# Two blocks' scores are held, their searches stand among the gathered rows, and the gates come two chunk pairs later

## The chip, the cores and the metric

The kernel runs on one core of one Trainium2 chip. The metric is the device time of one execution in microseconds (us), the median of three runs. The engines are named as in the profile: PE (TensorE), DVE (VectorE), ACT (ScalarE), POOL (GpSimd), SP (SyncE, which here issues the weights' transfers).

## What is computed

Two layers over 512 tokens of 1024 numbers, fp32. The first mixes by windowed attention and Fourier mixing, the second by a gated spatial unit; each is followed by an expert layer ("PEER"), and in this one the change lies:

```python
def peer_ffn(h, w_q, keys, u_tab, v_tab):
    # 512 tokens in blocks of 128; 8 heads, 2 sides, 128 keys a side, 16384 experts
    q = (xc @ w_q).reshape(PEER_BLOCK, PEER_HEADS, 2, PEER_KEY_DIM // 2)
    s = jnp.einsum("chsd,hskd->chsk", q, keys).astype(jnp.float32)
    top_s, top_i = lax.top_k(s, PEER_TOPK)                              # 16 of 128 a side
    cand = top_s[:, :, 0, :, None] + top_s[:, :, 1, None, :]
    best_s, best = lax.top_k(cand.reshape(...), PEER_TOPK)              # 16 of 256 pairs
    e = i1 * PEER_NKEYS + i2
    g = jax.nn.softmax(best_s, axis=-1)
    act = jax.nn.gelu(jnp.einsum("cd,chkd->chk", xc, u_tab[e]))
    return jnp.einsum("chk,chkd->cd", g * act, v_tab[e])
```

Each token uses 8 × 16 = 128 of the 16384 rows of `u_tab` and of `v_tab`.

## The kernel before

`peer_phase` builds one expert layer and is called twice. The 512 tokens are four blocks of 128. Blocks 0 and 1 are **gathered**: their rows are fetched from memory, 512 KB at a time. Blocks 2 and 3 are **dense**: for them PE multiplies by all experts, and a matrix of gates, zero nearly everywhere, picks out those that count.

**Asks.** For m = 0 to 15 (head and side) PE makes the query tile m of all four blocks (`ask(m)`, 24 matmuls) and then the scores: `score(m)` for blocks 0 to LATER−1, in one of two PSUM banks (L1243 and on), and `later_score(m)` for the last block. `score(m)` waits until DVE has replaced the found values of search m−2. DVE searches 16 of 128 twice: `top16(m)` takes blocks 0 to LATER−1 together, instruction by instruction; `later_top16(m)` takes the last block alone, from a copy that ACT made (`hold(m)`). Between searches DVE routes block 0 and part of block 1 (`route(b, step)`, 23 steps that find the best pairs and the experts' numbers; step 5 gives ACT the differences for the exponential of block b), and takes slots 0 to 7.

**Up.** For chunk c = 0 to 127 PE multiplies the two dense blocks by 128 experts' rows (`up(c)`), whose 512 KB come through a ring of three buffers that SP fills; ACT takes the result by `gelu(c)` into the matrix `gates`. `up(c)` waits for `gelu(c-2)`. After a pair of chunks p = c // 2 that stands in `EXP_AFTER`, ACT waits for the differences of a block and takes their exponential (L1553), in order with the gelus. After a pair in `TURN_AFTER` PE turns a dense block's weights, and DVE's `columns(b)` puts them where ACT can use them.

**Gates.** 32 groups of 8 tokens, 16 for each dense block. ACT makes one-hot rows (`one_hots`), PE multiplies them (`gates_of(g)`, L1300, at the pair in `GATES_AFTER`, one half behind each chunk), and the product, 8 × 128 × 128, says how much each expert counts. For chunks not yet computed ACT copies it into `gates` (`take_gates`, L1538), and gelus are later multiplied onto it (`post(p)` on DVE); for those already computed DVE multiplies (`spread(g)`, L1859). PSUM has room for two groups, so `gates_of(g)` waits for `spread(g-2)` and `take_gates(g-2)`.

**Down.** For c = 0 to 127 PE multiplies `gates` by the second table's rows (`down(c)`, L1310). It starts when all 32 groups are spread.

**Slots.** Beside all this DVE takes 512 slots, each one row per token for one block: 256 dots with `u_rows` (L1888) and 256 accumulations of `peer_v` rows (L1895). POOL fetches them by indirect transfers (L1134) into a dozen buffers and more; some (`EARLY`) lie in parts of `gates` that are not yet in use. What else DVE does after slot 7 is written out by slot numbers: behind slot i come `TOP_AT` (a single search), `ROUTE_AT`, `SOFTMAX_AT`, `COLUMNS_AT`, `SPREAD_AT` and `POST_AT`, in this order (L2050 to L2062). All engines run their instructions in program order. In layer 0, DVE's dense residual (L1960) stands between two of the last slots and opens the next layer's mixing; in layer 1 the last slots open the ending. The values of the tables before are in the diff.

Of the kernel before, what the change touches and what calls it, by code (L numbers as in the profile page):

```python
# [27 lines left out]
P = 128  # L28
# [19 lines left out]
FETCHED = 2  # L48
LATER = 3
PICKED = FETCHED * P  # L50
# [742 lines left out]
class Experts:  # L793


    def __init__(self, nc, room, l, split_at):
# [109 lines left out]
def peer_phase(nc, t, l, out_w, out_gate, xT, x_dram, hi, lo, ring, both, norm, ident, iota, one, gate, q,  # L906
               bridge=None, mixer=None, ending=None):

    with Room(nc, f"exp{l}") as r:
# [11 lines left out]
        FIRST_DOTS = 46  # L921
        EARLY = [(31, 0, 44), (39, 0, 60), (47, 0, 76), (55, 0, 88), (66, 60, 112), (74, 60, 128)]

        HEADS = [(0, 2), (2, 4), (4, PH)]
        ASK_ROUTE = {m: (0, range(8 * (m - 4), min(8 * (m - 4) + 8, STEPS))) for m in (4, 5, 6)}
        ASK_ROUTE.update({m: (1, range(8 * (m - 8), min(8 * (m - 8) + 8, STEPS))) for m in (8, 9, 10)})
        ASK_TOP = {1: 0, 2: 1, 3: 2, 7: 3}
        ASK_SLOTS = {11: (0, 1), 12: (2, 3), 13: (4, 5), 14: (6, 7)}
        SHIFT = 1 + ASK_SLOTS[14][1]
        FIRST_ROWS = 8  # L930

        GATES_AFTER = {13 + 3 * g // 2: g for g in range(GROUPS)}
# [15 lines left out]
        POST_AT = {SHIFT + (44 + 4 * (p - 14) if p <= 34 else 124 + 465 * (p - 34) // 100): p for p in POST}  # L948

# [230 lines left out]
        def _(pe):  # L1180
# [257 lines left out]
        def _(act):  # L1438
# [247 lines left out]
        def _(dve):  # L1686
# [349 lines left out]
            for i in range(SHIFT, SLOTS):  # L2036
# [6 lines left out]
                if ending and i == SLOTS - 3:  # L2043
# [203 lines left out]
```

## Time and profile before

| | |
|---|---|
| three runs | 2830.92, 2814.94, 2823.93 us |
| median | 2823.93 us |
| the profiled execution | 2829.58 us, its span 2827.5 us |
| PE busy | 2648.9 us, 94% |
| DVE busy | 2017.5 us, 71% |
| POOL busy | 1476.7 us, 52% |
| ACT busy | 1048.1 us, 37% |
| mean granted clock of PE | 0.976 |

All times of the trace count from the start of the span. The stages are, in layer 0 and layer 1:

| | layer 0 | layer 1 |
|---|---|---|
| up begins | 459 | 1790 |
| down begins | 979 | 2309 |
| PE's last tile down ends | 1450.5 | 2780.4 |
| last slot ends | 1511 | 2813 |

A row of a timeline gives the start, the length, the engine, the line, the operation, out<-in, how many of the same kind stand in a row, and in brackets the idle time before it with what ended it. A row of the view by lines gives busy time, mean length in ns and idle time before with what ended it. Since each engine works in order, the start of a row says when everything ahead of it on that engine was done.

### The profile page before, as it was taken

The numbers are of one execution on the slowest core, as the hardware profiler recorded it, in microseconds if no ns is written. First come the engines' busy times: TensorE is split into PE (matmuls) and PEld (weight loads), VectorE is DVE, ScalarE is ACT, GpSimd is POOL, SyncE is SP. The second block draws the span as 40 slices with busy tenths as digits, with TensorE's granted clock in tenths as the row PEclk, the third lists the DMA queues.
The fourth block names the chain that finished last, engine by engine and source line by source line (L and its number), as shares of the span: only waits on it lengthen the run. The fifth ranks groups of instructions, "written<-read, shape, count | busy, mean of one in ns | idle before, by whom it ended". The sixth has DMA issues, their size and how long they took to land. (4 is left out here: it accounts for less than half of the span.)

```text
span 2827.5 us, 37113 instructions
## 1 busy us (share of the span) xinstructions
PE 2648.9 (94%) x13042; PEld 2201.9 (78%) x13042; DVE 2017.5 (71%) x4301; ACT 1048.1 (37%) x2993; POOL 1476.7 (52%) x1122
## 2 busy tenths in 40 slices
PE   6899999999999999999978799999999999999996
PEld 4644687888888888888867778888888888888884
DVE  5463389988678756666677638998877775666667
ACT  4362331398888500000024432239878830000002
POOL 1000352656667745565647435365676774665554
PEclk9999999999999999999988999999999999999998
DMA  8282335999999999999985234699999999999997
GB/s 338 107 350 98 120 132 194 392 365 352 384 409 409 406 404 409 409 409 409 409 327 198 84 121 156 221 402 361 355 395 409 409 408 404 409 409 409 409 409 292
DMA packets 251625, 925.37 MB, mean 327 GB/s; under 512 B 27409, under 2 KB 35633, under 8 KB 244273
## 3 DMA queue, kind: packets, MB, share of 16 engines
q0 software_dynamic: 147456, 536.94, 48.4%
q1 hardware_dynamic: 99824, 381.88, 35.2%
q10 hardware_dynamic: 4160, 4.19, 0.4%
q8 instruction: 104, 1.70, 0.2%
q14 instruction: 81, 0.66, 0.1%
HBM read 916.61 MB, written 6.29 MB: 326 GB/s over the span
## 5 line engine op out<-in xcount | busy, mean ns | idle before, releaser
L1310 PE MATMUL exp_down<-peer_gates,all_ring 128*128 128x256 f32 x2720 | 612.8, 382 | 24.1 <-DMA all_ring<-in_peer_v 24.0
L1283 PE MATMUL exp_out<-peer_both,all_ring 128*128 128x256 f32 x2752 | 621.6, 382 | 7.8 <-DMA all_ring<-in_uT 5.1
L1310 PEld LDWEIGHTS exp_down<-peer_gates,all_ring 128*128 128x128 f32 x2720 | 509.4, 190 | 117.2 <-DMA all_ring<-in_peer_v 50.3
L1283 PEld LDWEIGHTS exp_out<-peer_both,all_ring 128*128 128x128 f32 x2752 | 519.6, 192 | 81.7 <-DMA all_ring<-in_uT 11.6
L1134 POOL DMA_INDIRECT all_xT<-in_u_rows,peer_eidx x278 | 365.9, 1316 | 157.0 <-DVE peer_dots L1888 91.2
L1895 DVE SCALAR_TENSOR_TENSOR peer_both<-all_xT,peer_dots,peer_both 128x1024 f32<-128x1024 f32 x226 | 299.9, 1327 | 148.1 <-DMA all_xT<-in_peer_v,peer_eidx 144.6
L1888 DVE CUSTOM_DVE_ANT_0 all_xT<-all_xT,peer_both 128x1024 f32<-128x1024 f32 x278 | 338.7, 1224 | 62.6 <-DMA all_xT<-in_u_rows,peer_eidx 61.2
L1134 POOL DMA_INDIRECT all_xT<-in_peer_v,peer_eidx x230 | 271.1, 1179 | 189.3 <-DVE peer_both L1895 156.7
L1310 PE MATMUL exp_down<-peer_gates,spare_ring 128*128 128x256 f32 x1376 | 315.1, 382 | 11.6 <-DMA spare_ring<-in_peer_v 11.5
L1521 ACT ACTIVATE spare_heavy<-all_iota_b,spare_index 128x128 f32<-128x128 bf16 x1024 | 314.3, 412 | 0.0
L1283 PE MATMUL exp_out<-peer_both,spare_ring 128*128 128x256 f32 x1344 | 304.8, 380 | 1.6 <-DMA spare_ring<-in_uT 1.5
L1895 DVE SCALAR_TENSOR_TENSOR peer_both<-late,peer_dots,peer_both 128x1024 f32<-128x1024 f32 x168 | 219.6, 1307 | 117.6 <-DMA late<-in_peer_v,peer_eidx 115.2
L1310 PEld LDWEIGHTS exp_down<-peer_gates,spare_ring 128*128 128x128 f32 x1376 | 257.6, 190 | 58.9 <-DMA spare_ring<-in_peer_v 25.0
L1283 PEld LDWEIGHTS exp_out<-peer_both,spare_ring 128*128 128x128 f32 x1344 | 251.2, 190 | 35.1 <-DMA spare_ring<-in_uT 3.6
L1134 POOL DMA_INDIRECT late<-in_peer_v,peer_eidx x168 | 189.7, 1129 | 142.7 <-DVE peer_both L1895 126.4
L1525 ACT ACTIVATE spare_heavy<-spare_heavy,spare_share 128x128 f32<-128x128 f32 x512 | 212.2, 503 | 0.0
L1607 ACT ACTIVATE bridge_w_hi<-bridge_raw 128x1024 fp32r<-128x1024 f32 x32 | 33.7, 1052 | 476.6 <-DMA bridge_raw<-in_w_gs_in 476.6
L1107 POOL TENSOR_TENSOR ask_w_lo<-ask_third,ask_w_hi 128x1024 fp32r<-128x1024 f32 x14 | 33.7, 2405 | 285.4 <-ACT ask_w_hi L1443 285.3
L1569 ACT ACTIVATE ending_gated<-exp_down,all_ada 128x256 f32<-128x256 f32 x8 | 3.0, 489 | 470.8 <-PE exp_down L1310 470.8
L1134 POOL DMA_INDIRECT peer_gates<-in_u_rows,peer_eidx x94 | 117.7, 1252 | 99.4 <-DVE peer_dots L1888 64.7
L125 PE MATMUL exp_down<-all_h_hi,ask_w_hi 128*128 128x512 f32 x352 | 145.2, 412 | 11.7 <-DVE ask_w_lo L1918 11.7
L1300 PEld LDWEIGHTS exp_down<-spare_heavy 128*128 128x128 f32 x1024 | 132.3, 192 | 26.4 <-ACT spare_heavy L1529 13.6
(323 smaller groups left out, 4161.8 us busy)
## 6 DMA issues: line engine op xcount, KB each, us to landing
all_ring<-in_uT SPq DMA_DIRECT2D x172, 512.0 KB, 6.8
all_ring<-in_peer_v SPq DMA_DIRECT2D x170, 512.0 KB, 6.8
mix_raw<-in_ada_tiles SPq DMA_DIRECT2D x48, 1024.0 KB, 10.3
spare_ring<-in_peer_v SPq DMA_DIRECT2D x86, 512.0 KB, 6.8
spare_ring<-in_uT SPq DMA_DIRECT2D x84, 512.0 KB, 6.8
bridge_raw<-in_w_gs_in SPq DMA_DIRECT2D x32, 512.0 KB, 3.5
all_ring<-in_w_peer_q SPq DMA_DIRECT2D x20, 512.0 KB, 3.4
ask_third<-in_w_peer_q SPq DMA_DIRECT2D x12, 512.0 KB, 3.5
```

The lines of the kernel that those rows point to most:

```text
L125: nc.tensor.matmul(out, w_hi, x_hi, start=first, stop=False)
L1107: nc.gpsimd.tensor_tensor(q.w_lo[m % 3][:, :, :], asked[m % 3][:, :, :], f32(q.w_hi[m % 3][:, :, :]), ALU.subtract).then_inc(s_lo, 1)
L1134: nc.gpsimd.indirect_dma_start(out=rows[j], out_offset=None, in_=t["u_rows"] if n < HALF else t["peer_v"], in_offset=bass.IndirectOffsetOn ...
L1283: mm = nc.tensor.matmul(outs[:, c % 2, 0:DENSE], raw[c % R][:, k, :], hd[:, k, :], start=(k == 0), stop=(k == KD - 1))
L1300: mm = nc.tensor.matmul(ps_g[g % 2][:, half * TG // 2 + k, :], heavy[:, 1, k, :], heavy[:, 0, k, :], start=True, stop=True)
L1310: mm = nc.tensor.matmul(dn[:, m, :], raw[at % R][:, m, :], gates[:, :, c, :], start=(c == 0 and m % 2 == 0), stop=(c == NKEYS - 1), skip_g ...
L1521: act.activation(heavy[:, side, k, :], iota[:, :, 0], ACT.Abs, scale=2.0, bias=q.index[:, b, side, first + k:first + k + 1]).then_inc(s_ap ...
L1525: act.activation(heavy[:, 0, k, :], heavy[:, 0, k, :], ACT.Relu, bias=q.share[:, b, 0, first + k:first + k + 1], scale=q.share[:, b, 1, fi ...
L1569: act.activation(ending.gated[:, m, :], dn[:, m, :], ACT.Copy, scale=gate[:, m:m + 1]).then_inc(s_egate, 1)
L1607: act.activation(bridge.w_hi[i % 3][:, :, :], bridge.raw[i % 3][:, :, :], ACT.Copy).then_inc(s_bhi, 1)
L1888: nc.vector.tensor_tensor_reduce(out=row, in0=row, in1=own[:, b, :], scale=1.0, scalar=0.0, op0=ALU.mult, op1=ALU.add, accum_out=q.dots[:, ...
L1895: nc.vector.scalar_tensor_tensor(out=acc[:, b, :], in0=row, scalar=q.dots[:, b, k:k + 1], in1=acc[:, b, :], op0=ALU.mult, op1=ALU.add).the ...
```

## The change

`LATER` falls from 3 to 2. `top16(m)` now searches blocks 0 and 1 only. The scores of blocks 2 and 3 are both held: `later_score(m)` is two matmuls, `hold(m)` two copies, and the new tensor `held` lies where `weighed` lay. `later_top16` takes the block as an argument, so there are 32 single searches in a layer in place of 16. Six of block 2's stand in the asks; its other ten are behind slots 8 to 17, and block 3's sixteen behind slots 42 to 57 (before: block 3's only, four in the asks and twelve behind every second slot of 33 to 55). Everything behind them moves: block 2's route from slots 8 to 30 to slots 18 to 40, its softmax from 31 to 41, its columns from 36 to 46, its spreads from 49, 54, 59 and so on to 61, 66, 71 and so on; block 3's first spread from 153 to 160 and its last from 255 to 262; block 1's route begins at slot 66 (58) and block 3's at 95 (90). On PE the gates of block 2 begin at pair 15 (13), those of block 3 at pair 39 (38). On ACT exp(0) stands after pair 0 (1) and exp(2) after pair 6 (4).

```diff
-LATER = 3
+LATER = 2
+        held = nc.alloc_sbuf_tensor_at(f"held{l}", [P, HS, NKEYS], F32, offset=weighed_at)
-        self.later_scores = later.sb("scores", [P, HS, NKEYS])
+        self.later_scores = [held, later.sb("scores", [P, HS, NKEYS])]
...
-        EARLY = [(31, 0, 44), (39, 0, 60), (47, 0, 76), (55, 0, 88), (66, 60, 112), (74, 60, 128)]
+        EARLY = [(31, 0, 44), (39, 0, 60), (47, 0, 76), (55, 0, 88), (66, 66, 112), (74, 66, 128)]
-        ASK_TOP = {1: 0, 2: 1, 3: 2, 7: 3}
+        ASK_TOP = {1: (2, 0), 2: (2, 1), 3: (2, 2), 7: (2, 3), 12: (2, 4), 13: (2, 5)}
-        GATES_AFTER = {13 + 3 * g // 2: g for g in range(GROUPS)}
-        GATES_AFTER.update({38 + 3 * g // 2: GROUPS + g for g in range(GROUPS)})
+        GATES_AFTER = {15 + 3 * g // 2: g for g in range(GROUPS)}
+        GATES_AFTER.update({39 + 3 * g // 2: GROUPS + g for g in range(GROUPS)})
-        EXP_AFTER = {1: 0, 4: 2, 20: 1, 28: 3}
-        TURN_AFTER = {9: 2, 33: 3}
+        EXP_AFTER = {0: 0, 6: 2, 20: 1, 28: 3}
+        TURN_AFTER = {11: 2, 34: 3}
-        ROUTE_AT = {SHIFT + n: (2, n) for n in range(STEPS)}
-        ROUTE_AT.update({SHIFT + 50 + 13 * n // 10: (1, n) for n in range(STEPS)})
-        ROUTE_AT.update({SHIFT + 82 + 13 * n // 10: (3, n) for n in range(STEPS)})
-        TOP_AT = {SHIFT + 25 + 2 * (m - 4): m for m in range(4, HS)}
-        SOFTMAX_AT = {SHIFT + 3: 0, SHIFT + 23: 2, SHIFT + 81: 1, SHIFT + 113: 3}
-        COLUMNS_AT = {SHIFT + 28: 2, SHIFT + 121: 3}
-        SPREAD_AT = {SHIFT + 41 + 5 * g + g * g // 15: g for g in range(GROUPS)}
-        SPREAD_AT.update({SHIFT + 145 + 68 * g // 10: GROUPS + g for g in range(GROUPS)})
+        ROUTE_AT = {SHIFT + 10 + n: (2, n) for n in range(STEPS)}
+        ROUTE_AT.update({SHIFT + 58 + 12 * n // 10: (1, n) for n in range(STEPS)})
+        ROUTE_AT.update({SHIFT + 87 + 13 * n // 10: (3, n) for n in range(STEPS)})
+        TOP_AT = {SHIFT + n: [(2, 6 + n)] for n in range(HS - 6)}
+        TOP_AT.update({SHIFT + 34 + n: [(3, n)] for n in range(HS)})
+        SOFTMAX_AT = {SHIFT + 3: 0, SHIFT + 33: 2, SHIFT + 86: 1, SHIFT + 118: 3}
+        COLUMNS_AT = {SHIFT + 38: 2, SHIFT + 128: 3}
+        SPREAD_AT = {SHIFT + 53 + 5 * g + g * g // 15: g for g in range(GROUPS)}
+        SPREAD_AT.update({SHIFT + 152 + 68 * g // 10: GROUPS + g for g in range(GROUPS)})
...
             def later_score(m):
...
-                score_block(m, LATER, later[m % 2]).then_inc(s_later_score, 1)
+                for i in range(NB - LATER):
+                    mm = score_block(m, LATER + i, later[m % 2][:, i, :])
+                mm.then_inc(s_later_score, 1)
...
             def hold(m):
                 act.wait_ge(s_later_score, m + 1)
-                act.activation(q.later_scores[:, m, :], later[m % 2], ACT.Copy).then_inc(s_held, 1)
+                for i in range(NB - LATER):
+                    last = act.activation(q.later_scores[i][:, m, :], later[m % 2][:, i, :], ACT.Copy)
+                last.then_inc(s_held, 1)
```

(`POST_AT` moves likewise, by 10 slots; `SHIFT` is 8, `STEPS` 23, `HS` and `GROUPS` 16.)

Three places in the order of instructions. The first is DVE in the asks of layer 0 at m = 12 (`top16`, and in the kernel after it `later_top16`): `exp_ps_t` is the PSUM tensor with the scores, `top_val` the found values. Before:

```order
L1709 MAX top_val<-exp_ps_t 128x8 x3
L1712 MAX_INDEX ask_idx<-top_val,exp_ps_t 128x8 x3
L1714 MATCH_REPLACE ask_kept<-top_val,exp_ps_t 128x128 x3
L1718 MAX top_val<-ask_kept 128x8 x3
L1721 MAX_INDEX ask_idx<-top_val,ask_kept 128x8 x3
L1723 CAST top_idx_2693<-ask_idx 128x3x32
```

After:

```order
L1716 MAX top_val<-exp_ps_t 128x8 x2
L1719 MAX_INDEX ask_idx<-top_val,exp_ps_t 128x8 x2
L1721 MATCH_REPLACE ask_kept<-top_val,exp_ps_t 128x128 x2
L1725 MAX top_val<-ask_kept 128x8 x2
L1728 MAX_INDEX ask_idx<-top_val,ask_kept 128x8 x2
L1730 CAST top_idx_2694<-ask_idx 128x2x32
L1737 MAX top_val<-held_2681 128x8
L1739 MAX_INDEX later_idx<-top_val,held_2681 128x8
L1740 MATCH_REPLACE later_kept<-top_val,held_2681 128x128
L1743 MAX top_val<-later_kept 128x8
L1745 MAX_INDEX later_idx<-top_val,later_kept 128x8
L1747 CAST top_idx_2694<-later_idx 128x32
```

The three-block search has become a two-block one, and behind six of the sixteen a search of six instructions for block 2 alone has come.

The second is DVE from slot 8 on (`ISA` is a slot's dot, the row with `peer_dots 128x1` its result), layer 0. Before, block 2's route starts at once:

```order
L1888 ISA spare_row,peer_dots<-spare_row,peer_both 128x1024
L1888 ISA peer_dots 128x1
L1759 TENSOR_TENSOR top_cand<-top_val 128x8x16
L1761 TENSOR_TENSOR top_cand<-top_val 128x8x56
L1764 TENSOR_TENSOR top_cand<-top_val 128x8x8
L1888 ISA all_xT,peer_dots<-all_xT,peer_both 128x1024
L1888 ISA peer_dots 128x1
L1769 MAX top_best<-top_cand 128x8 x8
```

After:

```order
L1895 ISA spare_row,peer_dots<-spare_row,peer_both 128x1024
L1895 ISA peer_dots 128x1
L1737 MAX top_val<-held_2681 128x8
L1739 MAX_INDEX later_idx<-top_val,held_2681 128x8
L1740 MATCH_REPLACE later_kept<-top_val,held_2681 128x128
L1743 MAX top_val<-later_kept 128x8
L1745 MAX_INDEX later_idx<-top_val,later_kept 128x8
L1747 CAST top_idx_2694<-later_idx 128x32
L1895 ISA all_xT,peer_dots<-all_xT,peer_both 128x1024
L1895 ISA peer_dots 128x1
```

Ten slots with a search of block 2 each have come ahead of its route.

The third is ACT at the start of the up stage of layer 0 (`exp_out` is PSUM with a chunk's result, `top_less` the differences). Before:

```order
L1501 ACT_TABLE_LOAD
L1501 ACTIVATE peer_gates<-exp_out 128x2x128 x4
L1553 ACT_TABLE_LOAD
L1553 ACTIVATE top_less<-top_less 128x128
L1501 ACT_TABLE_LOAD
L1501 ACTIVATE peer_gates<-exp_out 128x2x128 x6
L1553 ACT_TABLE_LOAD
L1553 ACTIVATE top_less<-top_less 128x128
L1501 ACT_TABLE_LOAD
L1501 ACTIVATE peer_gates<-exp_out 128x2x128 x15
```

After:

```order
L1508 ACT_TABLE_LOAD
L1508 ACTIVATE peer_gates<-exp_out 128x2x128 x2
L1560 ACT_TABLE_LOAD
L1560 ACTIVATE top_less<-top_less 128x128
L1508 ACT_TABLE_LOAD
L1508 ACTIVATE peer_gates<-exp_out 128x2x128 x12
L1560 ACT_TABLE_LOAD
L1560 ACTIVATE top_less<-top_less 128x128
L1508 ACT_TABLE_LOAD
L1508 ACTIVATE peer_gates<-exp_out 128x2x128 x15
```

The exponential of block 2 stands behind 14 gelus, where it stood behind 10.

## Rows read from the trace of the kernel before

**Rows 1.** By lines, PE, 371 to 460 us; then timeline, PE.
```profile
L1241 PE MATMUL exp_ps_t<-ask_keys,ask_qT 128*128 128x128 f32 x84 | 12.6, 288 | 6.6 <-DVE ask_kept L1714 6.6
...
410.04 0.83 PE L1241 MATMUL exp_ps_t<-ask_keys,ask_qT 128*128 128x128 f32 x6
...
1788.94 0.91 PE L1241 MATMUL exp_ps_t<-ask_keys,ask_qT 128*128 128x128 f32 x6 [0.55 <-DVE ask_kept L1714]
```

**Rows 2.** Timeline, PE, two tiles up of layer 0.
```profile
467.83 3.62 PE L1283 MATMUL exp_out<-peer_both,spare_ring 128*128 128x256 f32 x16
471.29 1.03 PE L1283 MATMUL exp_out<-peer_both,all_ring 128*128 128x256 f32 x4
```

**Rows 3.** Timeline, ACT, layer 0, the exponential of block 2.
```profile
499.54 0.31 ACT L1553 ACTIVATE top_less<-top_less 128x128 f32<-128x128 f32 x1 [2.19 <-DVE top_less L1775]
```

**Rows 4.** Timeline, DVE, the first spread of layer 0 and of layer 1.
```profile
567.06 0.38 DVE L1859 TENSOR_TENSOR peer_gates<-peer_gates,exp_down 128x224 f32<-128x224 f32 x1
...
1898.96 0.38 DVE L1859 TENSOR_TENSOR peer_gates<-peer_gates,exp_down 128x224 f32<-128x224 f32 x1
```

**Rows 5.** Timeline, PE, the third group of gates in both layers.
```profile
581.76 1.05 PE L1300 MATMUL exp_down<-spare_heavy 128*128 128x128 f32 x8
...
1913.43 1.05 PE L1300 MATMUL exp_down<-spare_heavy 128*128 128x128 f32 x8
```

**Rows 6.** By lines, DVE, 585 to 722 us; then timeline, spreads of groups 2 and 12.
```profile
L1859 DVE TENSOR_TENSOR peer_gates<-peer_gates,exp_down 128x272 f32<-128x272 f32 (+10 forms) x11 | 6.1, 558 | 22.4 <-ACT peer_gates L1538 22.4
...
590.84 0.44 DVE L1859 TENSOR_TENSOR peer_gates<-peer_gates,exp_down 128x272 f32<-128x272 f32 x1 [3.76 <-ACT peer_gates L1538]
...
719.34 0.69 DVE L1859 TENSOR_TENSOR peer_gates<-peer_gates,exp_down 128x512 f32<-128x512 f32 x1 [5.60 <-ACT peer_gates L1538]
```

**Rows 7.** Windows of L1895: window, us, DVE busy (x), clock, DMA, GB/s; timeline, last spread.
```profile
979.00:1450.00 471.00, 296.98 (x232) 1.00 1.03 408
...
976.54 1.17 DVE L1859 TENSOR_TENSOR peer_gates<-peer_gates,exp_down 128x976 f32<-128x976 f32 x1
```

**Rows 8.** Timeline, PE and DVE, both layers' ends; then window of L1895, DVE.
```profile
1446.91 3.62 PE L1310 MATMUL exp_down<-peer_gates,all_ring 128*128 128x256 f32 x16
...
1455.75 1.65 DVE L1960 SCALAR_TENSOR_TENSOR back<-exp_down,all_ada,back 128x256 f32<-128x256 f32 x4
...
2776.75 3.62 PE L1310 MATMUL exp_down<-peer_gates,all_ring 128*128 128x256 f32 x16
...
2780.40:2813.30 32.90, 28.42 (x21) 0.81 0.69 270
```

**Rows 9.** Timeline, DVE: searches in the asks, slot 8, a single search, layer 1.
```profile
381.74 0.68 DVE L1709 MAX8 top_val<-exp_ps_t 128x8 f32<-128x128 f32 x3
...
385.58 0.28 DVE L1730 MAX8 top_val<-later_scores 128x8 f32<-128x128 f32 x1
...
416.17 0.69 DVE L1709 MAX8 top_val<-exp_ps_t 128x8 f32<-128x128 f32 x3
...
483.37 1.22 DVE L1888 CUSTOM_DVE_ANT_0 spare_row<-spare_row,peer_both 128x1024 f32<-128x1024 f32 x1
...
530.73 1.22 DVE L1888 CUSTOM_DVE_ANT_0 peer_gates<-peer_gates,peer_both 128x1024 f32<-128x1024 f32 x1
...
531.88 0.29 DVE L1730 MAX8 top_val<-later_scores 128x8 f32<-128x128 f32 x1
...
533.67 1.22 DVE L1888 CUSTOM_DVE_ANT_0 peer_gates<-peer_gates,peer_both 128x1024 f32<-128x1024 f32 x1
...
1749.24 0.70 DVE L1709 MAX8 top_val<-exp_ps_t 128x8 f32<-128x128 f32 x3
...
1815.28 1.22 DVE L1888 CUSTOM_DVE_ANT_0 spare_row<-spare_row,peer_both 128x1024 f32<-128x1024 f32 x1
```

**Rows 10.** Timeline, PE, after a wait in the mixing; then its window, columns as above.
```profile
1480.20 0.58 PE L125 MATMUL exp_out<-bridge_h_hi,bridge_w_hi 128*128 128x256 f32 x1 [6.36 <-POOL bridge_w_lo L1160]
...
1480.20:1483.50 3.30, 3.30 (x15) 0.50 0.76 226
```

More of the change, by code:

```diff
@@ L812, in __init__ @@
         self.first_pick = asks.sb("first_pick", [P, PH // 2, TOPK, TOPK], BF16)
+        weighed_at = asks.at
         self.weighed = [asks.sb(f"weighed{j}", [P, KD, P]) for j in range(2)]
+        held = nc.alloc_sbuf_tensor_at(f"held{l}", [P, HS, NKEYS], F32, offset=weighed_at)
         self.moved = asks.sb("moved", [P, 2, 2])
@@ L930, in peer_phase @@
         FIRST_ROWS = 8
-        GATES_AFTER = {13 + 3 * g // 2: g for g in range(GROUPS)}
-        GATES_AFTER.update({38 + 3 * g // 2: GROUPS + g for g in range(GROUPS)})
+        GATES_AFTER = {15 + 3 * g // 2: g for g in range(GROUPS)}
+        GATES_AFTER.update({39 + 3 * g // 2: GROUPS + g for g in range(GROUPS)})
         DONE_AFTER = {g: 2 * p + 2 for p, g in GATES_AFTER.items()}
         WEIGH_AFTER = {p - 1: g for p, g in GATES_AFTER.items()}
-        EXP_AFTER = {1: 0, 4: 2, 20: 1, 28: 3}
-        TURN_AFTER = {9: 2, 33: 3}
-        ROUTE_AT = {SHIFT + n: (2, n) for n in range(STEPS)}
-        ROUTE_AT.update({SHIFT + 50 + 13 * n // 10: (1, n) for n in range(STEPS)})
-        ROUTE_AT.update({SHIFT + 82 + 13 * n // 10: (3, n) for n in range(STEPS)})
-        TOP_AT = {SHIFT + 25 + 2 * (m - 4): m for m in range(4, HS)}
-        SOFTMAX_AT = {SHIFT + 3: 0, SHIFT + 23: 2, SHIFT + 81: 1, SHIFT + 113: 3}
-        COLUMNS_AT = {SHIFT + 28: 2, SHIFT + 121: 3}
-        SPREAD_AT = {SHIFT + 41 + 5 * g + g * g // 15: g for g in range(GROUPS)}
-        SPREAD_AT.update({SHIFT + 145 + 68 * g // 10: GROUPS + g for g in range(GROUPS)})
+        EXP_AFTER = {0: 0, 6: 2, 20: 1, 28: 3}
[9 more added lines that the diff above has]
+        SPREAD_AT.update({SHIFT + 152 + 68 * g // 10: GROUPS + g for g in range(GROUPS)})
         POST = [p for p in range(PAIRS) if p > min(GATES_AFTER)]
-        POST_AT = {SHIFT + (44 + 4 * (p - 14) if p <= 34 else 124 + 465 * (p - 34) // 100): p for p in POST}
+        POST_AT = {SHIFT + (54 + 4 * (p - 16) if p <= 36 else 134 + 465 * (p - 36) // 100): p for p in POST}
         def known(p):
@@ L988, in peer_phase @@
         query = [dn[:, 2 * j:2 * j + 2, :].rearrange("p m n -> p (m n)") for j in range(2)]
-        later = [dn[:, 4 + 2 * j, 0:NKEYS] for j in range(2)]
+        later = [dn[:, 4 + 2 * j, :].rearrange("p (b n) -> p b n", n=NKEYS) for j in range(2)]
         turned = [outs[:, :, :].rearrange("p j n -> p (j n)"), dn[:, 4:8, :].rearrange("p m n -> p (m n)")]
@@ L1724, in top16, with later_top16 @@
                                                q.idx[:, :, :].unsqueeze(3).broadcast_to([P, LATER, TOPK, 2])))
-            def later_top16(m):
-                found, val = q.later_scores[:, m, :], q.val[:, LATER, m, :]
+            def later_top16(b, m):
+                found, val = q.later_scores[b - LATER][:, m, :], q.val[:, b, m, :]
                 dve.wait_ge(s_held, m + 1)
@@ L1739, in later_top16 @@
                 settled()
-                mark(nc.vector.tensor_copy(q.idx2[:, LATER, m % 2, m // 2, :, :],
+                mark(nc.vector.tensor_copy(q.idx2[:, b, m % 2, m // 2, :, :],
                                            q.later_idx[:, :].unsqueeze(2).broadcast_to([P, TOPK, 2])))
-                if m == HS - 1:
+                if (b, m) == (NB - 1, HS - 1):
                     settled()
@@ L1947, in _ @@
                 if m in ASK_TOP:
-                    later_top16(ASK_TOP[m])
+                    later_top16(*ASK_TOP[m])
                 if m in ASK_ROUTE:
@@ L2047, in _ @@
                     nc.vector.reciprocal(ending.rstd0[:, :], ending.rstd0[:, :]).then_inc(s_erstd0, 1)
-                if i in TOP_AT:
-                    later_top16(TOP_AT[i])
+                for b, m in TOP_AT.get(i, ()):
+                    later_top16(b, m)
                 if i in ROUTE_AT:
```

## The prediction

> **What bounds the kernel now.** I read the windows by stage, then waits at the seams of each expert layer. Both layers run the same program: the asks (16 tiles of queries and scores), 128 tiles up, 128 tiles down, and beside them 512 slots of gathered rows on VectorE (DVE).
>
> *Asks.* DVE searches without a pause while TensorE (PE) has to wait for it: 6.6 us in layer 0, 0.55 us before the last scores of layer 1 [rows 1]. PE's next tile starts when these scores are out, so DVE's searches are on the path in layer 0 and level with PE in layer 1.
>
> *Up stage, until the first spread.* PE sets the pace, one tile each 471.29 − 467.83 = 3.46 us [rows 2]. Three things come to it from DVE's slot table: the differences for exp(2) (ACT waits for them, and gelus queue behind it), the columns, and the spreads, since `gates_of(2)` on PE waits for `spread(0)`. In the trace exp(2) waits 2.19 us [rows 3]; `spread(0)` is 14.7 us ahead of `gates_of(2)` (567.06 against 581.76 us, 1898.96 against 1913.43) [rows 4, 5]. After it DVE is the early one: it waits 22.4 us for ACT's gates in 585 to 722 us, although it has done all it was given [rows 6].
>
> *Down stage.* DMA is full (share 1.03, 408 GB/s), and the rows come at 471 / 232 = 2.03 us a slot where DVE needs 1.3 [rows 7]. The last spread stands at 976.54 us, some 2 us ahead of the down stage, which begins at 979 [rows 7].
>
> *Ends.* Layer 0 ends by the slot that opens the dense residual: PE's last tile is done at 1446.91 + 3.62 = 1450.5, the residual starts at 1455.75 [rows 8]. Layer 1 ends by gathered rows: PE is done at 2780.4, then 21 accumulations take 28.42 us, 1.35 each [rows 8].
>
> **The change, part by part.** *Searches in the asks.* A search of three blocks takes 385.58 − 381.74 = 3.84 us [rows 9]. For two blocks the trace has no row; the bounds are 2/3 of it, 2.56, and all of it, 3.84. I take 2.75, near 2/3, since every instruction in it is one of three equal ones: −1.1 us each. A single search takes 533.67 − 531.88 = 1.79, and the dot ahead of it 531.88 − 530.73 = 1.15 [rows 9]. From the ninth search to slot 8 DVE takes 67.2 us in layer 0 and 66.0 in layer 1 [rows 9]. Now it is eight searches × −1.1 = −8.8, and two singles more × 1.79 = +3.6: −5.2. In layer 0 that search also starts when PE's scores are ready, 410.8, not at 416.17 [rows 1, 9]. Slot 8: 410.8 + 62.0 = 472.8 (10.6 earlier); layer 1: 1749.1 + 60.8 = 1809.9 (5.4 earlier). PE's asks lose their waits: −6.6 and −0.55. The extra score and copy per ask are the same four matmuls on PE and one more short copy on ACT, which has nothing else there: nothing.
>
> *Searches among the slots.* 26 stand there instead of 12; until the first spread it is 25 (slots 8 to 17, 42 to 56) instead of 8, and `spread(0)` stands 12 slots later. Before: 567.06 − 483.37 = 83.7 us from slot 8 [rows 4, 9]. Now 83.7 + 12 × 1.15 + 17 × 1.79 = 127.9. So `spread(0)` starts at 472.8 + 127.9 = 600.7 in layer 0 (33.6 later) and 1937.8 in layer 1 (38.8 later).
>
> *Gates two pairs later.* That is four tiles, 4 × 3.46 = 13.8 us. PE without a stall comes to `gates_of(2)` at 581.76 − 6.6 + 13.8 = 589.0 and 1913.43 − 0.55 + 13.8 = 1926.7 [rows 1, 2, 5]. `spread(0)` ends 0.4 after its start, at 601.1 and 1938.2: **12.1 and 11.5 us short**. Tables that gave 14.7 us of room now give none.
>
> *exp(2).* Its differences came 499.54 − 483.37 = 16.2 us behind slot 8 [rows 3, 9]. They now stand behind ten slots and ten searches more: 16.2 + 11.5 + 17.9 = 45.6, at 518.4 and 1855.5. Tile 16 needs the gelu that is queued behind exp(2), done about 2 us after the differences (estimated from the trace's function load and one gelu): 520.4 and 1857.5. Without a wait tile 16 would start at 467.83 + 14 × 3.46 − 6.6 = 509.7 [rows 2], and in layer 1, where up starts at about 1789.35, at 1844.7 [rows 1]. PE stands 10.7 and 12.8 us. This is not added to the 12.1 and 11.5: a PE that stood there comes to `gates_of(2)` at 599.7 and 1939.5, about when `spread(0)` ends. The two waits are one, and the longer rules: PE is late by −6.6 + 12.1 = +5.5 in layer 0 and −0.55 + 12.8 = +12.3 in layer 1.
>
> *Clock.* Behind 6.36 us of standing, 15 matmuls take 3.30 us at a granted clock of 0.50, 1.2 GHz [rows 10]; at 1.00 they would take half: about 1.6 us lost. Two such stops, the second partly inside the same wait: +1.8. For exp(1)'s differences (slot 72, some 11 slots and three spreads behind `spread(0)`, about 622, level with tile 41) I add 1. PE goes down **8.3 us later in layer 0 and 15.1 in layer 1**.
>
> The Trainium skill ("TensorE: Matmul & The Clock Gate", section "Part 1: The HAM clock gate") says that an idle array falls to 1.2 GHz and gets 2.4 GHz back only after sustained work. It speaks against this change, which puts stops into a stage that had none of this length; the trace agrees in kind (0.50 behind the 6.36 us).
>
> *Gathered rows.* From `spread(2)` at slot 59 to `spread(12)` at slot 118 a slot took (719.34 − 590.84) / 59 = 2.18 us, paced by the gates [rows 6]. The spreads stand 12 slots later, 26.1 us at that pace; the gates come 13.8 + 8.3 = 22.1 and 13.8 + 15.1 = 28.9 us later. The stream is thus 4.0 us ahead in layer 0 and 2.8 behind in layer 1, and the buffers have time to fill before. Bounds: no row gained, and 7 (the 14.7 us of room at 2.03). I take three rows in layer 0 and two in layer 1, near the low end. Block 3's spreads stand 7 slots later, its gates one pair: 14.2 us (at 2.03) against 6.9 + 8.3 or + 15.1, so the last spread stays about level with PE.
>
> *Sum.* Layer 0: PE's end 1450.5 + 8.3 = 1458.8 now decides, since the slot that opened the residual at 1455.75 comes no later: +3.1. Layer 1: while PE is at work a slot costs 2.03, after it 1.35, so 15.1 us more of PE leave 1 − 1.35 / 2.03 = 0.33 of it: +5.0; two rows gained: −2.7. Together +3.1 + 2.3 = **+5.4**. The profiled execution took 2829.58 (span 2827.5), 5.65 above the median 2823.93: 2835.0, or **2829** as a median.
>
> **The rivals.** *No change.* The stops are as forecast but made good: slot 491 had 5.2 us of room over PE, and more rows come during the stops. With four rows more in layer 1 (−5.4) and PE 5 late in layer 0 it is +0; about 2824. For it: DVE's 22.4 us of waiting, which the searches now fill. Against: that room lies after `spread(0)`, the stops before it.
>
> *Faster.* Searches are cheaper alone than I count. The low bound is a third of a three-block search, 1.28: 17 × 0.51 = 8.7 us, and with two-block searches at 2.56 another 1.5 us; PE then waits 2 us. PE keeps its 6.6, the slot stream the room. Layer 0: PE no longer waits, slot 491 comes by PE's end, −5.2; layer 1: eight rows (14.7 us and what the asks give) × 1.35 = −10.8. About 2824 − 16 = 2808. For it: DVE idles later. Against: the single searches wait on one another, and 1.79 is measured.
>
> *Slower.* Place: the seam from up to down, some 2 us wide [rows 7]. Block 3's spreads stand seven slots later at up to 2.03 us each, 14.2 us; the gates come one pair later. If DVE has gained no row by slot 118 and instead lags three (dots behind 26 searches, block 1 and 3's routes from slot 66 and 95 close behind), the last spread, slot 262, is 14.2 + 3 × 2.03 = 20.3 later, at 996.8, and done at 998, 19 behind the 979 of before. Layer 0: 19 − 5.2 = +14; layer 1: 19 × 0.33 + 3 × 1.35 = +10. About 2824 + 24 = 2848. It decides once DVE lags by more than those 2 us and PE's own delay. For it: a search more costs DVE 1.79 in a stage with 12 more of them. Against: 22.4 us of waits per layer to take it from. A two-block search as dear as three (3.84) leads here too: 8.8 us more on both stops.
>
> **How the numbers follow.** Forecast as worked out, 2829: 0.50. No change, 2824: 0.22. Faster, 2808: 0.13. Slower, 2848: 0.15. A measurement of this kernel tells 0.5% from no change, 14 us; so the first two are "same", 0.72, faster 0.13, slower 0.15. The range takes in both outer cases, with two us more on the side where all of layer 0's gain would show: 2806 to 2848.
>
> **What would show it.** Slot 8 at about 473 and 1810 us: the searches' price. ACT's exp(2) waiting some 15 us, and PE standing before tile 16: the exp step. PE's `gates_of(2)` at 601 and 1938 with little wait of its own: the two waits are one. DVE's waits for gates in 600 to 750 us falling from 22.4 to under 15: the cover. PE's first tile down at 987 in layer 0 (979 before), the last spread ahead of it. The dense residual at 1459, straight behind PE. In layer 1, 20 to 25 accumulations behind PE's last tile. I am wrong if PE does not stand before tile 16 or `gates_of(2)`, if the last spread comes behind PE's last tile up, or if the rows behind PE's end number under 15 or over 30.

## The result, and the profile after

The changed kernel takes 2846.68 us (median of five runs, 2845.17 to 2852.63) against 2823.93: the ratio is 1.0093, 95% interval 1.0079 to 1.0108. It is slower by 23 us. I had given "no measurable change" 0.72 and put the likeliest time at 2829. The measured time lies at the upper end of the stated range, 2806 to 2848, next to the rival "slower"; how much of that rival's mechanism was right is said below. The profiled execution took 2851.54 us (span 2849.5), 22.0 us more than that of the kernel before, so its trace holds the whole difference.

PE's waits in layer 0, by line, what they waited for, total, times, longest (the view of waits, kernel after, 340 to 1500 us):

```profile
PE exp_down L1315 <- DMA all_ring<-in_peer_v: 12.9, 17, 1.1
PE exp_out L1288 <- ACT peer_gates L1508: 11.9, 2, 10.2
PE exp_down L1315 <- DVE peer_gates L1866: 7.4, 1, 7.4
```

Two are new: 10.2 us before tile 16 and 7.4 us before the first tile down. The kernel after, timeline of PE and ACT, layer 0 (L1288 is `up`, L1315 `down`, L1560 the exponential):

```profile
520.34 0.31 ACT L1560 ACTIVATE top_less<-top_less 128x128 f32<-128x128 f32 x1 [14.22 <-DVE top_less L1782]
...
522.49 1.62 PE L1288 MATMUL exp_out<-peer_both,all_ring 128*128 128x256 f32 x3 [10.19 <-ACT peer_gates L1508]
...
993.05 5.88 PE L1315 MATMUL exp_down<-peer_gates,spare_ring 128*128 128x256 f32 x16 [7.40 <-DVE peer_gates L1866]
```

The last row is one tile: 5.88 us where a tile takes 3.62 [rows 8]. The window behind it shows why (us, PE busy, granted clock, DMA share, GB/s):

```profile
992.00:997.00 5.00, 3.95 (x9) 0.50 1.03 410
```

DVE in the kernel after: the ninth slot, the first spread of either layer, the last spread of layer 0. They answer to [rows 4], [rows 7] and [rows 9]:

```profile
474.82 1.22 DVE L1895 CUSTOM_DVE_ANT_0 spare_row<-spare_row,peer_both 128x1024 f32<-128x1024 f32 x1
...
602.94 0.42 DVE L1866 TENSOR_TENSOR peer_gates<-peer_gates,exp_down 128x256 f32<-128x256 f32 x1
...
1947.93 0.42 DVE L1866 TENSOR_TENSOR peer_gates<-peer_gates,exp_down 128x256 f32<-128x256 f32 x1
...
991.77 1.18 DVE L1866 TENSOR_TENSOR peer_gates<-peer_gates,exp_down 128x992 f32<-128x992 f32 x1
```

And DVE's waits for gates in 600 to 750 us (by lines), 22.4 in the kernel before [rows 6]:

```profile
L1866 DVE TENSOR_TENSOR peer_gates<-peer_gates,exp_down 128x256 f32<-128x256 f32 (+12 forms) x13 | 7.2, 558 | 2.5 <-ACT peer_gates L1545 2.5
```

To see where time comes in, I compared when the same instruction starts in two traces. Minus means earlier than in the kernel before; all in us.

| place | after | block 3's spreads back | stop alone, in the kernel before |
|---|---|---|---|
| layer 0, tile 0 up | −5.9 | −4.2 | −3.0 |
| tile 14 | −5.0 | +1.0 | +13.9 |
| tile 20 | +6.8 | +11.5 | +14.0 |
| tile 127 | +6.8 | +5.2 | +12.9 |
| first tile down | +14.3 | +5.5 | +12.9 |
| tile 8 down | +16.4 | +5.2 | +12.7 |
| last tile down | +17.6 | +7.3 | +13.0 |
| dense residual | +12.5 | +2.2 | +11.8 |
| layer 1, tile 0 up | +8.2 | −0.3 | +10.6 |
| tile 127 | +19.4 | +11.0 | +26.3 |
| first tile down | +26.3 | +11.8 | +26.3 |
| last tile down | +28.9 | +11.0 | +26.6 |
| last slot | +22.1 | +11.3 | +27.3 |

In the kernel after each layer gets about 12 us at the stop before tile 16, another 7 at the seam, and about 2 at the low clock behind it. Rows get ahead of PE while it stands at the seam: slot 491 of layer 0 comes 9.2 us earlier than in the kernel before, with block 3's spreads back 0.9 later. So the ends give some back: layer 0's residual stood 5.2 us behind PE's end and stands straight behind it now, the mixing behind it takes 4.4 us less (+12.5 becomes +8.2), and layer 1 has fewer rows left behind PE:

```profile
2809.30:2835.30 26.00, 14.79 (x11) 0.91 0.33 127
```

This window of L1902 in the kernel after answers to the one of [rows 8]: 11 accumulations where there were 21. DVE then waits 7.4 us for the ending's scale, which comes from PE's last tile over ACT (the view of waits, 2809 to 2836 us):

```profile
DVE ending_rstd L2052 <- ACT ending_rstd L1596: 7.4, 1, 7.4
```

So the end of layer 1 hung on gathered rows before, and hangs on PE's last tile now.

### The profile page after: what moved, and what is told of

Read it like the earlier page. It is cut to its first block and busy times, and to the rows that moved or that the text cites. A ratio compares the mean times of both kernels' runs of the same rounds, so it can differ in the third digit from the quotient of the medians.

```text
span 2849.5 us, 37189 instructions
## 1 busy us (share of the span) xinstructions
PE 2654.3 (93%) x13042; PEld 2197.8 (77%) x13042; DVE 2036.2 (71%) x4329; ACT 1052.3 (37%) x3021; POOL 1434.9 (50%) x1122
## 5 line engine op out<-in xcount | busy, mean ns | idle before, releaser
L1288 PE MATMUL exp_out<-peer_both,all_ring 128*128 128x256 f32 x2752 | 626.9, 382 | 30.3 <-ACT peer_gates L1508 23.2
L1315 PE MATMUL exp_down<-peer_gates,all_ring 128*128 128x256 f32 x2720 | 612.4, 382 | 22.6 <-DMA all_ring<-in_peer_v 22.4
L1315 PEld LDWEIGHTS exp_down<-peer_gates,all_ring 128*128 128x128 f32 x2720 | 508.7, 190 | 115.8 <-DMA all_ring<-in_peer_v 47.9
L1288 PEld LDWEIGHTS exp_out<-peer_both,all_ring 128*128 128x128 f32 x2752 | 515.8, 191 | 105.8 <-issue 24.7
L1137 POOL DMA_INDIRECT all_xT<-in_u_rows,peer_eidx x280 | 349.7, 1249 | 203.6 <-DVE peer_dots L1895 149.9
L1902 DVE SCALAR_TENSOR_TENSOR peer_both<-all_xT,peer_dots,peer_both 128x1024 f32<-128x1024 f32 x228 | 302.5, 1327 | 153.5 <-DMA all_xT<-in_peer_v,peer_eidx 149.0
L1895 DVE CUSTOM_DVE_ANT_0 all_xT<-all_xT,peer_both 128x1024 f32<-128x1024 f32 x280 | 340.2, 1220 | 61.8 <-DMA all_xT<-in_u_rows,peer_eidx 60.5
L1315 PE MATMUL exp_down<-peer_gates,spare_ring 128*128 128x256 f32 x1376 | 319.7, 386 | 28.5 <-DMA spare_ring<-in_peer_v 14.6
L1315 PEld LDWEIGHTS exp_down<-peer_gates,spare_ring 128*128 128x128 f32 x1376 | 260.0, 192 | 78.8 <-DMA spare_ring<-in_peer_v 29.3
L1288 PE MATMUL exp_out<-peer_both,spare_ring 128*128 128x256 f32 x1344 | 304.1, 379 | 1.4 <-ACT peer_gates L1516 1.3
L1902 DVE SCALAR_TENSOR_TENSOR peer_both<-late,peer_dots,peer_both 128x1024 f32<-128x1024 f32 x168 | 219.5, 1307 | 108.3 <-DMA late<-in_peer_v,peer_eidx 105.2
L1288 PEld LDWEIGHTS exp_out<-peer_both,spare_ring 128*128 128x128 f32 x1344 | 252.8, 190 | 35.1 <-issue 1.7
L1305 PE MATMUL exp_down<-spare_heavy 128*128 128x128 f32 x1024 | 137.9, 278 | 13.0 <-issue 7.8
```

Of the source, the lines that this page charges most:

```text
L1137: nc.gpsimd.indirect_dma_start(out=rows[j], out_offset=None, in_=t["u_rows"] if n < HALF else t["peer_v"], in_offset=bass.IndirectOffsetOn ...
L1288: mm = nc.tensor.matmul(outs[:, c % 2, 0:DENSE], raw[c % R][:, k, :], hd[:, k, :], start=(k == 0), stop=(k == KD - 1))
L1305: mm = nc.tensor.matmul(ps_g[g % 2][:, half * TG // 2 + k, :], heavy[:, 1, k, :], heavy[:, 0, k, :], start=True, stop=True)
L1315: mm = nc.tensor.matmul(dn[:, m, :], raw[at % R][:, m, :], gates[:, :, c, :], start=(c == 0 and m % 2 == 0), stop=(c == NKEYS - 1), skip_g ...
L1895: nc.vector.tensor_tensor_reduce(out=row, in0=row, in1=own[:, b, :], scale=1.0, scalar=0.0, op0=ALU.mult, op1=ALU.add, accum_out=q.dots[:, ...
L1902: nc.vector.scalar_tensor_tensor(out=acc[:, b, :], in0=row, scalar=q.dots[:, b, k:k + 1], in1=acc[:, b, :], op0=ALU.mult, op1=ALU.add).the ...
```

## The experiments

Ratios are against the kernel before, measured again beside each variant; its medians there were 2821.8 to 2824.4 us.

**The seam undone.**

```diff
-        SPREAD_AT.update({SHIFT + 152 + 68 * g // 10: GROUPS + g for g in range(GROUPS)})
+        SPREAD_AT.update({SHIFT + 145 + 68 * g // 10: GROUPS + g for g in range(GROUPS)})
```

> The changed kernel with one table entry undone: block 3's spreads stand behind slots 153 to 255 again, not 160 to 262. Seam theory (the last spread, paced by rows that come at 2.03 us a slot, holds PE's first tile down): PE's wait there falls from 7.4 us to under 1, layer 0 goes down at about 985.5 instead of 993.05, PE ends both down stages 8 to 9 us earlier, the whole is 2831 (2828 to 2835). Stop theory (PE's stop of 10.2 us before tile 16 is what costs): nothing of the 22.8 us comes back, 2846 +- 4.

Measured: 2839.38 us, ratio 1.0059 (1.0037 to 1.0081); profiled span 2838.8, 10.7 under that of after. PE has no wait for the last spread; down begins at 984.28. Seven slots of one table are worth 7.3 us by the medians (5.2 if each is taken against the kernel before measured beside it) and 10.7 by the profiles, as the seam theory wants in sign and place, though less than the 15 it gave. The stop before tile 16 (9.1 us) is left, and now layer 1 loses by it 11.6 us from first tile to last slot.

**The seam added to the kernel before**: the same entry the other way, 145 to 152.

> The kernel before with one table entry changed: block 3's spreads stand behind slots 160 to 262. Seam theory: last spread 14 us later, at about 990.7, PE waits about 12 us for it, goes down at about 992 at half clock for a few us, residual of layer 0 about 10 us later, layer 1's end 7 to 8 later still: 2841 (2836 to 2846). Stop theory: no stop is added before the spreads, so 2824 to 2827.

Measured: 2863.3 us, 1.0145 (1.0120 to 1.0170). Far more than expected. PE's waits in layer 0 (view of waits, 400 to 1500 us; L1300 is `gates_of`) and one of them:

```profile
PE exp_down L1300 <- issue: 19.4, 6, 8.3
...
792.27 1.62 PE L1300 MATMUL exp_down<-spare_heavy 128*128 128x128 f32 x6 [8.27 <-issue]
```

Here `gates_of(18)` stands where it stood while `spread(16)`, which it waits for, comes at 791.37 and takes 0.80 us, seven slots later; and so on with five more groups. The view names no releaser for these waits; that it is the spread follows from the program and from the times. The last spread then comes no later than PE does, and there is no wait at the seam. In the changed kernel the gates stand one pair later; PE waits only 5.5 us of this kind in layer 0 (3.5 in the kernel before), and the seven slots are felt at the seam instead. The price of slots depends on which of the two waits PE meets.

**The stop moved away, the seam left.** Block 3's searches behind slots 62 to 77, exp(2) and the turn later:

```diff
-        EARLY = [(31, 0, 44), (39, 0, 60), (47, 0, 76), (55, 0, 88), (66, 66, 112), (74, 66, 128)]
+        EARLY = [(31, 0, 44), (39, 0, 60), (47, 0, 76), (55, 0, 88), (66, 84, 112), (74, 84, 128)]
-        EXP_AFTER = {0: 0, 6: 2, 20: 1, 28: 3}
-        TURN_AFTER = {11: 2, 34: 3}
+        EXP_AFTER = {0: 0, 9: 2, 20: 1, 28: 3}
+        TURN_AFTER = {13: 2, 34: 3}
-        TOP_AT.update({SHIFT + 34 + n: [(3, n)] for n in range(HS)})
+        TOP_AT.update({SHIFT + 54 + n: [(3, n)] for n in range(HS)})
```

> The changed kernel without its stop: block 3's single searches stand behind slots 62 to 77 instead of 42 to 57 (28.6 us less ahead of the first spread), exp(2) after pair 9 and the turn after pair 13, block 3's spreads stay at slots 160 to 262. Seam theory: PE's wait before tile 16 (10.2) goes, its last tile up ends 11 to 13 us earlier, and the wait for the last spread grows from 7.4 to about 19; down still begins at about 993, the whole stays at 2846 +- 4. Stop theory: 10 us a layer come back, 2826 to 2830.

Measured: 2869.1 us, 1.0169 (1.0148 to 1.0189), 22 slower than after; both theories missed it. The wait before tile 16 did go, but the searches now stand between the spreads, and PE and ACT wait there (waits of PE in 400 to 1500 us, of ACT in 600 to 700):

```profile
PE exp_down L1305 <- issue: 14.6, 8, 5.6
...
PE exp_down L1315 <- DVE peer_gates L1866: 7.1, 1, 7.1
...
ACT top_less L1560 <- DVE top_less L1782: 10.7, 1, 10.7
```

The seam's 7.1 stayed as it was, since rows and spreads fell back together.

**Both at once**: the last edit and the spreads back at 145.

> Both at once: no stop (block 3's searches behind slots 62 to 77, exp(2) after pair 9, turn after pair 13) and block 3's spreads back behind slots 153 to 255. Seam theory: the last spread stands at 976 to 977 as in the kernel before, PE waits 4 to 6 us for it and goes down at about 978 to 980; the 6.6 us from the asks are lost there; 2824 (2818 to 2829), level with the kernel before. Stop theory: as without the seam, 2826 to 2830, no better than the same kernel with the late spreads.

Measured: 2852.89 us, 1.0109 (1.0089 to 1.0128). Not level with before: the expectation failed with its premise, that moving the searches would free PE. Against the last kernel the seam is worth 16.2 us here.

**The stop moved, no search moved** (seam undone, `EXP_AFTER` 6 to 9, `TURN_AFTER` 11 to 13).

> The kernel with block 3's spreads back at slots 153 to 255, and besides exp(2) after pair 9 (was 6) and the turn of block 2 after pair 13 (was 11); no search is moved. If the stop before tile 16 and a stop for the first spread are one and the same lateness of DVE (as the prediction had it), the wait before tile 16 (9.1 us) goes and PE waits 8 to 14 us at the gates of group 2 for the first spread instead; down begins within 1 us of where it did (984.3 in layer 0), 2839 +- 4. If the exponential's place is the cause by itself, PE is 9 us earlier and the time is 2828 to 2832.

Measured: 2840.58 us, 1.0070 (1.0042 to 1.0098), the same as the 2839.38 with the stop in its old place. The wait before tile 16 is gone; in its place PE waits for the first spread before the gates of group 2:

```profile
601.18 1.19 PE L1305 MATMUL exp_down<-spare_heavy 128*128 128x128 f32 x4 [6.43 <-issue]
```

Its other waits for gates in that stretch make up a part (2.5 us for the one-hots of group 0). That the exponential and the spread show one lateness of DVE, and not two costs, holds, with a wait of 6.4 where I gave 8 to 14: from the first tile up to the last tile down PE loses 11.2 and 11.4 us in the two layers, against 11.5 and 11.4 with the stop in its old place.

**The searches left out.** The 26 single searches among the slots are not made; their results are zeros, set once. First with the spreads late, then with the spreads back.

```diff
+            mark(nc.vector.memset(q.val[:, LATER:NB, :, :], 0.0))
+            mark(nc.vector.memset(q.idx2[:, LATER:NB, :, :, :, :], 0.0))
...
                 for b, m in TOP_AT.get(i, ()):
-                    later_top16(b, m)
+                    if (b, m) == (NB - 1, HS - 1):
+                        settled()
+                        dve.sem_inc(s_later, 1)
```

> The changed kernel without the 26 single searches among the slots (that part of the computation is left out, their results are zeros set once), everything else in its place, block 3's spreads at slots 160 to 262. DVE loses 46 us of work a layer. Seam theory in its strict form (only the slot number of the last spread counts, since rows are paced by DMA): PE has no stop in the up stage and waits 10 to 18 us for the last spread; down begins at 988 to 993 in layer 0; 2838 to 2846. Search theory (the searches' time is the cost, wherever the spreads stand): PE's stop and the seam wait both go, 2818 to 2826.

> The same without the 26 searches, and block 3's spreads back at slots 153 to 255. If the loss of the change is the sum of two things, the seam (7 slots) and DVE's 17 more searches before the first spread (PE's stop), neither is left: level with the kernel before or up to 8 us below it, 2814 to 2824. If it is over 2830, something else in the change costs, for instance the gates standing later on PE.

Measured: 2836.18 us, 1.0043 (1.0030 to 1.0057), and 2820.68 us, 0.9993 (0.9980 to 1.0006). The seam stands alone in the first, the second has neither. The start of the down stage in the first and in the second:

```profile
984.53 1.19 PE L1315 MATMUL exp_down<-peer_gates,spare_ring 128*128 128x256 f32 x2 [7.37 <-DVE peer_gates L1866]
```

```profile
975.52 1.75 PE L1315 MATMUL exp_down<-peer_gates,spare_ring 128*128 128x256 f32 x7 [0.74 <-DVE peer_gates L1866]
```

The four kernels make a table, medians in us, with the spans of the profiles in brackets:

| | spreads at 160 to 262 | at 153 to 255 | the seam |
|---|---|---|---|
| 26 searches among the slots | 2846.7 (2849.5) | 2839.4 (2838.8) | 7.3 (10.7) |
| none of them | 2836.2 (2834.3) | 2820.7 (2821.7) | 15.5 (12.6) |
| the searches | 10.5 (15.2) | 18.7 (17.1) | both: 26.0 (27.8) |

By the medians either cause would hide 8 us of the other, but the upper two kernels were each measured apart from the lower two, and single runs of the one with 2839.4 reach from 2831.9 to 2848.2. The traces show no hiding. PE's wait at the seam in layer 0 is 7.40 us with the searches and 7.37 without. From the first tile up to the last tile down the seam adds 12.0 us in layer 0 and 9.4 in layer 1 with the searches, 11.2 and 8.4 without; the searches add 10.6 and 10.2 with the seam, 9.8 and 9.3 without. In each layer the two add up: 8 to 12 us for the seam, 9 to 11 for the searches.

Without both the kernel is level with the one before. That bounds what the gates' later place and the held scores cost, but not at nothing: this variant also lacks the 12 searches that the kernel before makes among its slots, 12 × 1.79 = 21.5 us of DVE's time in a layer, and they may cover a cost. A variant with the old number of searches there was not run.

**The stop alone, in the kernel before.**

```diff
-        EXP_AFTER = {1: 0, 4: 2, 20: 1, 28: 3}
+        EXP_AFTER = {1: 0, 2: 2, 20: 1, 28: 3}
```

> The kernel before with one number changed: exp(2) stands after pair 2 (chunk 5) in place of pair 4, so that ACT waits for DVE's differences as in the changed kernel; PE stands about 13 us before tile 8 and nothing else is moved. By the prediction's term (a late PE costs layer 1 a third, layer 0 what exceeds 5.2 us): +8 + 4 = +12, 2834. If rows do not come faster while PE stands, since their buffers are full then, layer 1 pays in full: +8 + 13 = +21, 2843. If the stop is made good in the up stage: under +4.

Measured: 2850.81 us, 1.0096 (1.0069 to 1.0123): +26.5, above all three. The stop came out at 15.5 us, not 13. It is lost nearly whole in each layer: the last column of the table of shifts stays at +13 through layer 0 (from −3) and at +26 through layer 1 (from +10.6), and the slots run with it (slot 100: +13.6, slot 300: +12, slot 491: +11.8). DVE's own slots explain that (timelines of PE and DVE; `columns(2)`, L1849, waits for PE's turn; the last row is the last spread of layer 0, 12.8 us later than in [rows 7]):

```profile
499.53 2.04 PE L1283 MATMUL exp_out<-peer_both,spare_ring 128*128 128x256 f32 x4 [15.51 <-ACT peer_gates L1501]
...
545.73 0.43 DVE L1849 TENSOR_SCALAR spare_index<-exp_ps_t 128x256 f32<-128x256 f32 x1 [8.90 <-PE exp_ps_t L1290]
...
989.38 1.17 DVE L1859 TENSOR_TENSOR peer_gates<-peer_gates,exp_down 128x976 f32<-128x976 f32 x1
```

The columns and the spreads stand between the slots, in order, so a late PE holds the slots too: slot 18 is still 2.2 us early, slot 40 is 6.8 late and slot 60 13.5. From there on the shift stays, and no rows run ahead. DVE's waits for ACT's gates before the down stage, 22.4 us in all in the kernel before, are not used up by it: here they are 23.2.

**An attempt at the end of layer 0**: `BRIDGE_FROM = SLOTS - 21` to `SLOTS - 24`, in the kernel before.

> The kernel before with one number changed: the dense residual of layer 0 stands three slots earlier (behind slot 488 in place of 491). In the trace of before it starts at 1455.75, 5.2 us behind PE's last tile down; three slots are 6.1 us. If those slots are what holds it, it starts at 1450 to 1451, layer 1 begins 4 to 5 us earlier and the whole is 2819 to 2820 against 2824. If the rows that are passed stand in the way later (POOL's fetches, the mixing stage), nothing comes of it: 2824 +- 2.

Measured: 2823.61 us, 1.0001 (0.9986 to 1.0015). The residual starts straight behind PE:

```profile
1445.27 0.88 DVE L1960 SCALAR_TENSOR_TENSOR back<-exp_down,all_ada,back 128x256 f32<-128x256 f32 x2 [2.26 <-PE exp_down L1310]
```

It starts 10.5 us earlier than in [rows 8] (its layer had begun 8.2 earlier), layer 1 begins 4.3 earlier, and the span is 2826.0 against 2827.5. Nothing comes of it, and the trace shows where the gain goes, in the mixing between the layers:

```profile
1475.88 0.58 PE L125 MATMUL exp_out<-bridge_h_hi,bridge_w_hi 128*128 128x256 f32 x1 [10.25 <-POOL bridge_w_lo L1160]
```

The same matmul starts at 1480.20 in [rows 10], behind a wait of 6.36. PE had come to the mixing's first product 8.5 us earlier (1459.49 against 1467.98), then waits 3.9 longer for POOL, and is 4.3 earlier behind it, as is the last slot. The residual's place is not what holds layer 1's start there; POOL's `bridge_w_lo` is. No kernel here beats the one before.

## Why the prediction was wrong, point by point

**Slot 8 and the price of searches: right, but for 2 us.** Slot 8 was forecast at 472.8 and came at 474.82. A two-block search takes 2.59 us from 375.29 to 377.88 (forecast 2.75), a single one 1.79 as before; DVE waited 6.8 us in layer 0 for scores before its two-block searches, 3.4 before the three-block ones, which I had not counted.

**PE's gain in the asks: mostly not there.** I took −6.6 us for PE's waits in layer 0. From its first scores to its first tile up the kernel before takes 102.6 us in layer 0 and 95.3 in layer 1; in the three variants of it that leave the asks alone, it is 95.2 to 95.3 in five of six layers and 105.7 in one. The changed kernel takes 94.6 wherever I looked. So the steady gain is 0.7 us, and the 6.6 was an event, of a kind that came in two of eight layers. [rows 1] showed it truly, but it was one layer of one execution, and layer 1 of the same trace (0.55) spoke against counting on it. The table of shifts counts from the trace with the event, so its first row (−5.9) is no steady gain either.

**exp(2) and the first spread: right in place and size.** The wait at the exponential was forecast at about 15 and is 14.22; PE's stop 10.7 and is 10.19; the first spread 600.7 and is 602.94. In layer 1 the stop was forecast at 12.8 and is 10.25. That the stop and the gates are one lateness is shown by the kernel that moved it.

**The seam: the step that failed first.** "Block 3's spreads stand 7 slots later, its gates one pair: 14.2 us against 6.9 + 8.3 or + 15.1, so the last spread stays about level with PE." The 14.2 is right: the spreads of block 3 come 13.3 to 15.0 us late from group 18 to 30 in layer 0, and the last one 15.2. The 6.9 has no place in it. A pair at which gates stand moves work within the up stage and does not make the stage end later; PE was 6.8 us late at its last tile up. The room was smaller than I read, too: the last spread of [rows 7] ends at 977.71, so 1.0 us before the first tile down at 978.75, and not 2. What is left, 15.2 − 6.8 − 1.0 = 7.4, is the wait in the trace, 7.40; PE's first tile down, forecast at 987, starts at 993.05. In layer 1 the wait is 6.57.

The rival "slower" named this seam, and was given 0.15. That its 2848 lies so near has luck in it. It let DVE fall three rows behind at slot 118, which did not come (the shift there is +2.5 us), put the last spread 20.3 us late where it was 15.2, and counted layer 1 at +10 where it was +13.9.

**The rows ahead: there were none in layer 0.** I had the stream three rows ahead there. At slots 124 to 255 the shift against the kernel before is between −1 and +2.8 us: rows in both come as DMA brings them. In layer 1 the same slots are 3.6 to 7.6 us later, counted from the layer's first tile up. What I took for gain was used up by the searches before slot 124: 22.4 us of DVE's waits became 2.5.

**What a late PE costs: sized too low.** The sum gave layer 1 a third of its 15.1 and layer 0 what exceeded 5.2 us of room. The stop alone shows that a stop in the up stage is paid nearly in full in either layer, since slots and tiles move together: a stop with 15.5 us of wait became 13.6 by the start of layer 1 and another 16.8 by its last slot. In the changed kernel layer 1 alone took +13.9 instead of +2.3. The 11 accumulations behind PE's last tile, where I had forecast 20 to 25, are under the 15 that I had named as a sign of being wrong.

**The clock: right in kind.** The first tile down runs at 0.50 and takes 5.88 us for 3.62. Behind the stop the granted clock is 0.50 as well, from 522.4 to 526 us; PE loses 11.8 us between tile 14 and tile 20, of which 10.2 are the wait; the rest, 1.6 us, is about what I had put down for the low clock (1.8 for two stops). By the Trainium skill ("TensorE: Matmul & The Clock Gate", "Part 1: The HAM clock gate") an idle array falls to 1.2 GHz; the trace agrees at the seam, with a granted clock of 0.50.

**The sum.** +5.4 was forecast. Measured at the same points: layer 0 +12.5 at its residual instead of +3.1, of which 8.2 were left when layer 1 began; layer 1 +13.9 instead of +2.3.

## What to carry to other kernels

When a table of slot numbers is shifted, price it in time at every place where another engine waits for the entry, above all at the end of a stage; and compare it with how late that engine itself will be there, not with how far its own entries were moved in its order. Where engines wait for each other in program order at many places, a stop is not absorbed by idle time that lies later: look for room ahead of the first such wait. A wait that one layer of a trace shows and its twin does not can be an event, and is no gain to count on before a second trace shows it.

## What was not expected of the hardware

A short DVE instruction can take thirty times its length while POOL works without a pause. In the kernel before, layer 0, the timelines of DVE and POOL:

```profile
423.03 5.48 DVE L1775 TENSOR_TENSOR top_less<-top_best 128x32 f32<-128x32 f32 x1
...
421.36 2.40 POOL L1107 TENSOR_TENSOR ask_w_lo<-ask_third,ask_w_hi 128x1024 fp32r<-128x1024 f32 x1
423.70 4.75 POOL L1107 TENSOR_TENSOR ask_w_lo<-all_ring,ask_w_hi 128x1024 fp32r<-128x1024 f32 x2
```

The same instruction, in a variant whose asks are the same, with POOL's subtractions apart:

```profile
419.28 0.17 DVE L1775 TENSOR_TENSOR top_less<-top_best 128x32 f32<-128x32 f32 x1
```

The long one ends at 428.51, POOL's row of two at 428.45. Fetches had kept POOL busy until 421.3, so three subtractions stood in a row. The same holds of other short instructions, for instance this one, usually 0.18 us, which ends 0.04 us behind POOL's subtraction:

```profile
373.07 2.42 DVE L1740 CAST top_idx<-later_idx 128x32 bf16<-128x32 uint32 x1
...
373.06 2.39 POOL L1107 TENSOR_TENSOR ask_w_lo<-ask_third,ask_w_hi 128x1024 fp32r<-128x1024 f32 x1 [3.00 <-ACT ask_w_hi L1443]
```

That the two engines' operations exclude each other is the likeliest reading; no run here took POOL's work away to show it.

The 5.48 us are not by themselves what made PE wait 6.6 us in [rows 1]. The same instruction took 4.61 us in layer 1 of that trace, and 4.79 and 4.60 in the two layers of the last variant, and the asks took the usual 95.3 there; in the other slow layer, of 105.7, it took 0.17. What the two slow layers share, and the other six lack, are four earlier instructions of DVE, in layer 0 of the kernel before at 373, 381, 387 and 392 us, that take 2.42, 0.88, 1.04 and 2.37 us for 0.17 to 0.18 each; DVE is 5.5 us late behind them. Each ends 0.03 to 0.04 us behind a subtraction of POOL. Why their starts fall together there and not in the other layers stays open.

The kernel before varies by itself about as much as some variants differ from it: 2813.5 to 2832.1 us over all its runs. With the intervals reached here, effects under some 4 us could not be told.
